# Three more pairs of each down-projection sweep on seven products, their sums formed during attention

## What is computed

```python
h = rms_norm(x, ln1[l]);  p = h @ w_in[l]
r_out = retention(rq, rk, rv, rg, ret_gn[l])
s_out = swa_sink_attention(sq, sk, sv, sinks[l])
x = x + concatenate([r_out, s_out]) @ w_out[l]
h = rms_norm(x, ln2[l]);  u = h @ w_ffn_in[l];  a, b = split(u, 2)
a = causal_depthwise_conv(a, conv_w[l], conv_b[l])
x = x + (gelu(a) * b) @ w_ffn_out[l]          # w_ffn_out: 5632 x 2048
return rms_norm(x, ln_f)
```

## Time and profile before

| | us |
|---|---|
| median of 3 runs | 1091.36 |
| lowest and highest | 1090.43, 1093.61 |
| the profiled execution, its own time | 1090.57 |
| its span, first to last instruction | 1088.8 |
| TensorE busy in the span | 1075.9 |
| VectorE busy | 834.0 |
| ScalarE busy | 600.8 |

### The profile page before, as it was taken

How to read it: one execution, slowest core, us unless ns; L and a number is a source line. 1 busy time by engine, 2 the same in 40 slices (tenths; PEclk the granted TensorE clock), 3 DMA queues, 4 the chain that set the end, 5 groups by cost and what they waited for, 6 DMA issues and landing times.

```text
span 1088.8 us, 16760 instructions
## 1 busy us (share of the span) xinstructions
PE 1075.9 (99%) x5777; PEld 920.4 (85%) x5777; DVE 834.0 (77%) x1126; ACT 600.8 (55%) x806; POOL 80.4 (7%) x85
## 2 busy tenths in 40 slices
PE   8999999999999999999999999999999999999996
PEld 7888888888888888888888888888888888888885
DVE  6755777666668577968879678686788988898898
ACT  7445555555555454544545445455454777767773
POOL 2000111111100000101101011010010100000000
PEclk9999999999999999999999999999999999999999
DMA  9766555555599678797897887978877599869992
GB/s 346 263 190 194 159 170 157 157 171 166 164 325 351 177 267 311 225 337 253 281 324 230 317 269 253 351 213 320 283 238 276 178 315 323 305 231 311 328 334 81
DMA packets 163352, 276.06 MB, mean 254 GB/s; under 512 B 9091, under 2 KB 77537, under 8 KB 159984
## 3 DMA queue, kind: packets, MB, share of 16 engines
q1 hardware_dynamic: 162448, 273.39, 75.5%
q0 software_dynamic: 544, 1.69, 0.4%
q10 hardware_dynamic: 320, 0.47, 0.1%
HBM read 248.18 MB, written 27.26 MB: 253 GB/s over the span
## 4 chain that ended last, share of the span: by engine, by line
PE 97%; DVE 1%; DMA 0%; ACT 0%; issue 0%; DVEq 0%; ACTq 0%
PE acc L702 16%; PE acc L610 12%; PE acc L612 12%; PE acc L611 12%; PE acc L710 8%; PE bank_s L702 8%; PE bank_tr L702 8%; PE bank_tr L710 4%; PE bank_s L710 4%; PE bank_s L612 2%; PE bank_s L610 2%; PE bank_s L611 2%; PE bank_tr L612 1%; PE bank_tr L611 1%; PE bank_tr L610 1%; PE bank_s L758 0%
## 5 line engine op out<-in xcount | busy, mean ns | idle before, releaser
L973 ACT ACTIVATE w_hi<-raw 128x1024 fp32r<-128x1024 f32 x292 | 309.5, 1061 | 404.5 <-PE acc L612 135.7
L1259 DVE TENSOR_TENSOR w_lo<-raw,w_hi 128x1024 fp32r<-128x1024 f32 x292 | 356.1, 1224 | 186.5 <-ACT w_hi L973 185.6
L702 PE MATMUL acc<-h_both,w_hi 128*128 128x512 f32 x768 | 238.5, 392 | 0.0
L702 PEld LDWEIGHTS acc<-h_both,w_hi 128*128 128x128 f32 x768 | 137.9, 189 | 23.2 <-DVE rstd_row L1647 0.2
L710 PE MATMUL acc<-h_both,w_lo 128*128 128x256 f32 x768 | 154.2, 282 | 0.0
L710 PEld LDWEIGHTS acc<-h_both,w_lo 128*128 128x128 f32 x768 | 125.9, 191 | 7.5
L702 PE MATMUL bank_s<-h_both,w_hi 128*128 128x512 f32 x384 | 118.6, 390 | 0.0
L702 PE MATMUL bank_tr<-h_both,w_hi 128*128 128x512 f32 x384 | 118.6, 390 | 0.0
L610 PE MATMUL acc<-w_hi,h_both 128*128 128x512 f32 (+1 forms) x288 | 111.9, 389 | 1.0 <-DVE h_both L1273 1.0
L612 PE MATMUL acc<-w_hi,h_both 128*128 128x512 f32 (+1 forms) x288 | 109.0, 378 | 0.0
L611 PE MATMUL acc<-w_lo,h_both 128*128 128x512 f32 (+1 forms) x288 | 108.8, 378 | 0.0
(11 more groups left out here) (275 smaller groups left out, 1713.9 us busy)
## 6 DMA issues: line engine op xcount, KB each, us to landing
raw<-in_w_ffn_in SPq DMA_DIRECT2D x176, 512.0 KB, 4.3
raw<-in_w_in SPq DMA_DIRECT2D x130, 256.0 KB, 3.0
raw<-in_w_ffn_out SPq DMA_DIRECT2D x64, 512.0 KB, 6.2
stage<-in_w_ffn_out SPq DMA_DIRECT2D x24, 1024.0 KB, 8.3
kept_sums<-stage SPq DMA_DIRECT2D x24, 1024.0 KB, 6.5
raw<-kept_sums SPq DMA_DIRECT2D x24, 768.0 KB, 6.2
raw<-in_w_out SPq DMA_DIRECT2D x32, 512.0 KB, 4.9
raw<-in_w_in SPq DMA_DIRECT2D x19, 512.0 KB, 9.3
```

The costliest lines, as they stand in the source:

```text
L702: ins = mm(banks[ft // 2][:, ft % 2, :], w_hi[:, slot, q * COLS + ft * P:q * COLS + (ft + 1) * P], h_both[:, 2 * k + q, :, :].rearrange("p ...
L973: run(w_hi[:, n % SPLIT, :], raw[:, n % RAW, :], ACT.Copy).then_inc(hi_ready, 1)
L1259: tt(w_lo[:, n % SPLIT, :], raw[:, n % RAW, :], w_hi[:, n % SPLIT, :].bitcast(F32), ALU.subtract).then_inc(lo_ready, 1)
```

## The change

- A third set of seven-product pairs, 5, 11 and 17 of each sweep. The pattern of a sweep before is two seven pairs, one eight pair, from pair 3 to pair 19. Now the seven pairs are 3 to 7, 9 to 13 and 15 to 19; pairs 8 and 14 stay between the runs of five.
- Their weight sums are formed in attention steps 0 to 5, one pair and sweep per step, in a new buffer `head_stage` (number 4 of `staging`). SP loads it (1 MB) and stores it; its loop over the heads is written out for this (`head_traffic`). VectorE does the four subtractions behind its sixth and seventh tile of the step.
- `kept_sums` holds five blocks of a pair instead of four, so all stores grow from 1.0 to 1.25 MB, and a seven pair loads its first slot as one transfer of 512 KB from `kept_sums` (rows of 4 KB) instead of two of 256 KB.
- `token_sums` runs over three sets; ScalarE's and VectorE's rows of the new seven pairs gain `g_sums` and `t_hi`/`t_lo` rows.
- The scratch for GpSimd's own transfers is 4096 instead of 8192 bytes.

```diff
 FIRST_SET = list(range(3, 19, 3))
 SECOND_SET = list(range(4, 20, 3))
+THIRD_SET = [5, 11, 17]
+S_SETS = [FIRST_SET, SECOND_SET, THIRD_SET]
+HEAD_STAGED = [(sweep, p) for sweep in range(2) for p in THIRD_SET]
+HEAD_BUFFER = 4
...
                     if is_seven(r) and half == 0:
                         kept = kept_sums[kept_index(sweep, p)]
-                        sp.dma_start(raw[:, slot, 0:COLS], w_ffn_out_v[:, 2 * p, c0:c0 + COLS]
-                                     ).then_inc(raw_landed[slot], 16)
-                        sp.dma_start(raw[:, slot, COLS:2 * COLS], kept[:, 0:COLS]).then_inc(raw_landed[slot], 16)
+                        sp.dma_start(raw[:, slot, :], kept[:, 0:2 * COLS]).then_inc(raw_landed[slot], 16)
...
-                             stage[:, j, 1:5, :].rearrange("p c n -> p (c n)")).then_inc(stage_stored[j], 16)
+                             staging(j).rearrange("p c n -> p (c n)")).then_inc(stage_stored[j], 16)
...
+            def head_traffic(n):
+                step, k = divmod(n - HEAD_TILE, 8)
+                store, fetch = step - 3, step - 2
+                if k == 3 and 0 <= store < len(HEAD_STAGED):
+                    stage_store(HEAD_BUFFER, 0, store, kept_index(*HEAD_STAGED[store]))
+                if k == 6 and 0 <= fetch < len(HEAD_STAGED):
+                    if fetch:
+                        sp.wait_ge(stage_stored[HEAD_BUFFER], 16 * fetch)
+                    sweep, p = HEAD_STAGED[fetch]
+                    stage_load(HEAD_BUFFER, sweep, 2 * p)
...
+                    def split(k):
+                        lo(ahead + 8 * j + k, i, 16)
+                        if k in (5, 6):
+                            stage_sums(HEAD_BUFFER, i, 2, j, k - 5)
...
-                step, set_ = divmod(k, 2)
-                pairs = (FIRST_SET, SECOND_SET)[set_]
+                step, set_ = divmod(k, len(S_SETS))
+                pairs = S_SETS[set_]
...
-    nc = bacc.Bacc("TRN2", target_bir_lowering=False, num_devices=1, dynamic_dma_scratch_size=8192)
+    nc = bacc.Bacc("TRN2", target_bir_lowering=False, num_devices=1, dynamic_dma_scratch_size=4096)
```

More of the change, by code:

```diff
@@ L81 @@
 SECOND_SET = list(range(4, 20, 3))
[L82 to L86, removed]
+THIRD_SET = [5, 11, 17]
+S_SETS = [FIRST_SET, SECOND_SET, THIRD_SET]
+S_PAIRS = sorted(sum(S_SETS, []))
+S_SLOT = {pair: i for i, pair in enumerate(sum(S_SETS, []))}
+S_SUMS = 4 * len(S_SETS)
+HEAD_STAGED = [(sweep, p) for sweep in range(2) for p in THIRD_SET]
+HEAD_BUFFER = 4
+STAGE_USES = (11, 11, 1, 1, len(HEAD_STAGED))
 OUT_STAGED = [(0, 4), (1, 4), (0, 7), (1, 7)]
@@ L122, in kept_index @@
 def kept_index(sweep, p):
-    return 2 * SET * (p in SECOND_SET) + SET * sweep + (FIRST_SET if p in FIRST_SET else SECOND_SET).index(p)
+    own = [p in pairs for pairs in S_SETS].index(True)
+    return 2 * sum(map(len, S_SETS[:own])) + len(S_SETS[own]) * sweep + S_SETS[own].index(p)
 def raw_use(pair):
@@ L150, in down_raw_plan @@
         slots_of[pair] = first
-        count[first] += 32 if is_seven(pair) else 16
+        count[first] += 16
         count[first + 1] += 16
@@ L282, in build, with staging @@
         rstd_row = sb("rstd_row", [P, SEQ])
+        def staging(j):
+            return head_stage[:] if j == HEAD_BUFFER else stage[:, j]
         def pair_hi(r):
@@ L545, in _ @@
             sp.dma_start(v_shift[64:128, :], kv_tok[0:64, 1, v0:]).then_inc(shift_landed, 16)
[L546 to L550, removed]
+            def head_traffic(n):
[8 more added lines that the diff above has]
+                    stage_load(HEAD_BUFFER, sweep, 2 * p)
+            for n in range(HEAD_TILE, OUT_TILE):
+                load_head(n, n % RAW, (n - HEAD_TILE) // 8, (n - HEAD_TILE) % 8)
+                head_traffic(n)
             def store_out_staged(n):
@@ L1509, in attention_step, with stage_sums @@
                 mix_out(s, pair)
+            def stage_sums(j, f, each, use, part):
+                b11, b12, b21, b22, fresh = (staging(j)[:, i, :] for i in range(5))
+                if part == 0:
+                    dve.wait_ge(stage_landed[j], f * (16 * each) + 16 * (use + 1))
+                    tt(fresh, b22, b12, ALU.subtract).then_inc(stage_summed[j], 1)
+                    tt(b12, b12, b11, ALU.subtract).then_inc(stage_summed[j], 1)
+                else:
+                    dve.wait_ge(stage_summed[j], f * (4 * each) + (4 * use + 2))
+                    tt(b22, b22, b12, ALU.subtract).then_inc(stage_summed[j], 1)
+                    dve.wait_ge(stage_summed[j], f * (4 * each) + (4 * use + 3))
+                    tt(b21, b21, b22, ALU.subtract).then_inc(stage_summed[j], 1)
             ahead = HEAD_TILE + 8 + SPLIT
-            with dve.Fori(0, RET_HEADS // 2 - 1) as i:
+            with dve.Fori(0, len(HEAD_STAGED) // 2) as i:
                 for j in range(2):
-                    attention_step(i * 2 + j, j, i + 4 * j, lambda k: lo(ahead + 8 * j + k, i, 16))
-            for s in (RET_HEADS - 2, RET_HEADS - 1):
+                    def split(k):
+                        lo(ahead + 8 * j + k, i, 16)
+                        if k in (5, 6):
+                            stage_sums(HEAD_BUFFER, i, 2, j, k - 5)
+                    attention_step(i * 2 + j, j, i + 4 * j, split)
+            for s in range(len(HEAD_STAGED), RET_HEADS):
                 attention_step(s, s % 2, s // 2 + 4 * (s % 2), lambda k: lo(ahead + 8 * s + k))
```

36 lines of the change are left out of this document (14 added, 22 removed).

## The result

| | us |
|---|---|
| kernel before, median of 6 runs | 1091.69 |
| changed kernel, median of 6 runs (1100.23 to 1103.28) | 1101.49 |
| ratio, 95% interval | 1.009 [1.008, 1.0101] |
| profiled execution of the changed kernel, and its span | 1101.72, 1099.9 |

The change made the kernel 9.8 us slower. The prediction said 1089.9 (1086.5 to 1094) and gave slower a chance of 0.16.

A forecast was written before the change was run, and what follows sets the result against it. TensorE, busy 1075.9 of 1088.8 us, was taken as the bound. 1090.57 - 4.08 (matmuls removed) + 1.7 (VectorE's tail) + 1.3 (late transfers) = 1089.5 us profiled, given as 1089.9 for the median; range 1086.5 to 1094.

The forecast's parts named there:

- Two places in HBM that looked like 280 and 404 GB/s: Down projection: w_ffn_out blocks at 280 GB/s, kept_sums at 404, so the larger kept_sums transfer saves 0.29 us per seven pair.

The follow-up runs named there:

- e5: Changed kernel with two separate buffers for sums, eight slots for blocks only, next blocks asked for first, activation sums of only six pairs: 1088.41 us, ratio 0.9965.
- e2: Changed kernel with a seven pair's second slot also loaded from kept_sums, same bytes: 1101.03 us, ratio 1.009.
- e4: Changed kernel with a seven pair's first slot loaded as two 256 KB transfers, from w_ffn_out and kept_sums: 1101.5 us, ratio 1.0094.

## What to carry to other kernels

Before more is sent through a ring of buffers, work out the round of one buffer (request, landing, each reader until it is free) and set it against the time in which the ring comes round, the number of buffers over the buffers used per step, times the step's time. A rate in GB/s says nothing of this, and a margin of 0.3 us shows only as small harmless waits. Where one queue serves two kinds of transfer, ask first for the one whose round is tightest: with blocks three pairs deep that alone was 10 us here, while with four pairs deep the same order of the program cost nothing (e5). When an edit moves an instruction, see which transfer or which shared port moves with it.

## What was not expected of the hardware

- 312 to 328 GB/s in the changed kernel became 351 to 356 for the same reads when they were asked for earlier (e5).
- Two places in HBM that looked like 280 and 404 GB/s in windows of 3 us make no difference that can be told when exchanged (e2, e4).
- A GpSimd multiplication of 128x512 (9.71 us for four) made the VectorE subtraction beside it 1.10 us longer, whether that was 0.55 or 2.28 us long. The kernel before had it already: the longest subtraction on `stage` took 1787 ns against 685, 1.10 us more, and the subtraction at 448.82 us that took 1.78 us lay beside GpSimd's `conv` (448.52 to 450.05). The Trainium skill, SBUF — State Buffer, Who interferes with whom, has it that a VectorE instruction with two inputs in SBUF contends with a GpSimd one that reads SBUF; the trace agrees that they contend, at 1.10 us each time, where one GpSimd multiplication took 2.4.
